# A two-block transformer kernel on one core: the split weights of every stage placed 64 bytes further on in their buffers

## The reference, cut to what matters

```
for l in range(DEPTH):                                   # DEPTH = 2
    h = rmsnorm(x, mix_norm[l]);  p = h @ w_in[l]        # 1024 x 1440
    x = x + mixers(p) @ w_o[l]                           # 1024 x 1024
    h = rmsnorm(x, ffn_norm[l])
    x = x + (silu(h @ w_gate[l]) * (h @ w_up[l])) @ w_down[l]   # 1024 x 2816, 2816 x 1024
...
# second model, for the context (256 rows) and for the latents (512 rows)
y = mixer_ab(modulate(h))          # h @ ab_w_in (4112 columns) ... @ ab_w_out
h = (silu(g) * u) @ ffn_w_out      # g, u = split(h @ ffn_w_in), 2816 wide, per layer
y = mixer_c(...)                   # h @ attn_w_qkv, joint attention, @ attn_w_out
```

## Time and profile before

| | us |
|---|---|
| runs | 3002.12, 3000.85, 3006.8 |
| median | 3002.12 |
| the profiled execution | 3006.76 |
| its span in the trace | 3004.9 |
| PE busy in the span | 2942.4 (98%) |
| POOL, DVE, ACT busy | 1310.1, 1824.1, 1265.7 |

### The profile page before, as it was taken

One profiled execution on the slowest core, in us unless ns is written; L12 is line 12 of the kernel. 1 busy time (PEld: TensorE's weight loads), 2 busy tenths in 40 slices (PEclk: granted clock), 3 DMA queues, 4 the chain that ended last, 5 costly groups with the idle time before them and its releaser, 6 DMA issues.

```text
span 3004.9 us, 43067 instructions
## 1 busy us (share of the span) xinstructions
PE 2942.4 (98%) x16850; PEld 2479.0 (82%) x16850; DVE 1824.1 (61%) x3001; ACT 1265.7 (42%) x2026; POOL 1310.1 (44%) x687
## 2 busy tenths in 40 slices
PE   8999999999999999999999999999999999999999
PEld 7668888786788888778888998878788788889998
DVE  5656777856563553655327867666775567474445
ACT  4643222246444333225336655542223435454445
POOL 4323444532276334333444454444444330176665
PEclk9999999999999999999999999999999999999999
DMA  7224554522245223223333433445554210123332
GB/s 136 67 65 123 172 174 148 178 62 74 75 134 151 88 71 91 78 69 110 116 105 93 117 116 112 140 127 169 182 171 131 96 64 11 43 64 106 99 106 78
DMA packets 468697, 323.92 MB, mean 108 GB/s; under 512 B 90264, under 2 KB 435488, under 8 KB 467984
## 3 DMA queue, kind: packets, MB, share of 16 engines
q1 hardware_dynamic: 463728, 309.55, 35.0%
q0 software_dynamic: 2112, 5.32, 0.6%
q10 hardware_dynamic: 2656, 6.30, 0.6%
HBM read 315.85 MB, written 5.24 MB: 107 GB/s over the span
## 4 chain that ended last, share of the span: by engine, by line
PE 88%; DVE 7%; POOL 2%; ACT 2%; issue 1%; DMA 1%; POOLq 0%; DVEq 0%; ACTq 0%
PE G L3350 13%; PE G L3359 10%; PE G L3360 10%; PE G L3364 10%; PE G L3606 4%; PE G L3607 4%; PE G L3611 4%; PE G L3627 2%; PE G L3631 2%; PE G L3628 2%; PE G L4687 1%; PE G L3674 1%; PE G L3669 1%; PE G L3670 1%; POOL WL L844 1%; PE G L3379 1%
## 5 line engine op out<-in xcount | busy, mean ns | idle before, releaser
L844 POOL TENSOR_TENSOR WL<-raw,WH 128x1024 fp32r<-128x1024 f32 (+2 forms) x454 | 1051.7, 2338 | 1491.0 <-ACT WH L925 1491.0
L925 ACT ACTIVATE WH<-raw 128x1024 fp32r<-128x1024 f32 (+2 forms) x454 | 431.8, 999 | 471.9 <-PE G L3611 304.9
L3359 PE MATMUL G<-hH,WH 128*128 128x512 f32 x1216 | 476.9, 392 | 0.7 <-ACT xtok L1783 0.7
L3360 PE MATMUL G<-hL,WH 128*128 128x512 f32 x1216 | 473.6, 389 | 0.0
L1997 DVE SCALAR_TENSOR_TENSOR acc<-adaw,cvec,acc 128x512 f32<-128x512 f32 x280 | 285.8, 1073 | 4.2
L3364 PE MATMUL G<-hH,WL 128*128 128x512 f32 x1216 | 287.9, 389 | 0.0
L3359 PEld LDWEIGHTS G<-hH,WH 128*128 128x128 f32 x1216 | 228.2, 188 | 52.7 <-issue 3.3
L3364 PEld LDWEIGHTS G<-hH,WL 128*128 128x128 f32 x1216 | 228.2, 188 | 47.4
L3360 PEld LDWEIGHTS G<-hL,WH 128*128 128x128 f32 x1216 | 228.3, 188 | 46.6
L2026 DVE TENSOR_TENSOR FH<-silu,G 128x512 fp32r<-128x512 f32 x44 | 30.3, 688 | 233.6 <-PE G L3364 178.1
L896 POOL TENSOR_TENSOR WL<-raw,WH 128x512 fp32r<-128x512 f32 x101 | 129.4, 1298 | 85.5 <-ACT WH L1048 85.4
(11 more groups left out here) (887 smaller groups left out, 6919.8 us busy)
## 6 DMA issues: line engine op xcount, KB each, us to landing
raw<-ffn_w_in_in SPq DMA_DIRECT2D x264, 256.0 KB, 3.4
adaw<-ada_w_in SPq DMA_DIRECT2D x48, 1024.0 KB, 5.2
raw<-ab_w_in_in SPq DMA_DIRECT2D x128, 256.0 KB, 3.0
raw<-ffn_w_out_in SPq DMA_DIRECT2D x96, 256.0 KB, 3.0
raw<-w_gate_in SPq DMA_DIRECT2D x88, 256.0 KB, 3.3
raw<-w_up_in SPq DMA_DIRECT2D x88, 256.0 KB, 3.4
raw<-w_down_in SPq DMA_DIRECT2D x64, 256.0 KB, 2.9
raw<-w_in_in SPq DMA_DIRECT2D x40, 256.0 KB, 3.4
```

Source lines behind the costliest of these rows:

```text
L844: nc.gpsimd.tensor_tensor(low(c)[:, cut], raw[c % 2][:, cut], high(c)[:, cut].bitcast(F32), ALU.subtract)\
L925: nc.scalar.activation(high(c)[:, cut], raw[c % 2][:, cut], ACT.Copy).then_inc(weights_hi, 1)
L3359: mm(dst, view(high(c), k), xh, start=(k == 0 and not (joint and i)), stop=False)
L3360: mm(dst, view(high(c), k), xl, start=False, stop=False)
```

## The change

All chunks, in every stage, lie at columns 16 to 2063 of their buffers. `high` and `low` lose their case, the table `beside` goes, the blocks of the last feed-forward (`block_of`) move by `SIDE`, and the three places that named `WH` and `WL` directly go through `high` and `low`. What is written there (ACT's copies, POOL's and DVE's differences) and what is read (PE's stationary operands, or moving ones where the factors are exchanged) moves by 64 bytes; `raw`, the transfers, the activations and all results stay where they are. Every engine has the same instructions with the same waits in the same order as before: 10,020 matmuls, 513 ACT copies, 494 POOL and 19 DVE subtractions have another address in them, and the chunks of `c` and `k` have none.

```diff
         def block_of(buffers, c, b):
 
             i = turn_of[c, b]
-            return buffers[(seven_from + i // 4) % 2][:, i % 4 * BLOCK:i % 4 * BLOCK + BLOCK]
+            return buffers[(seven_from + i // 4) % 2][:, SIDE + i % 4 * BLOCK:SIDE + i % 4 * BLOCK + BLOCK]
...
-        beside = {first[name] + i for name, n, _ in names if name[0] in "ck" for i in range(n)}
 
         def high(c):
-            return WH[c % 2][:, SIDE:SIDE + SLOT] if c in beside else WH[c % 2][:, 0:SLOT]
+            return WH[c % 2][:, SIDE:SIDE + SLOT]
 
         def low(c):
-            return WL[c % 2][:, SIDE:SIDE + SLOT] if c in beside else WL[c % 2][:, 0:SLOT]
+            return WL[c % 2][:, SIDE:SIDE + SLOT]
...
-                    for j, (x, y) in enumerate(((WH, hH), (WH, hL), (WL, hH))):
-                        last = mm(G[b][:, :], view(x[c % 2], k), y[:, k, :], start=(k == NH // 2 and j == 0), stop=(k == NH // 2 - 1 and j == 2))
+                    for j, (x, y) in enumerate(((high(c), hH), (high(c), hL), (low(c), hH))):
+                        last = mm(G[b][:, :], view(x, k), y[:, k, :], start=(k == NH // 2 and j == 0), stop=(k == NH // 2 - 1 and j == 2))
...
```

More of the change, by code:

```diff
@@ L4503, in last_out @@
                 for q in range(KD):
-                    for j, (x, y) in enumerate(((WH, hH), (WH, hL), (WL, hH))):
-                        last = mm(out_bank(n, k)[:, :], view(x[c % 2], q), y[:, q, :], start=(q == 0 and j == 0), stop=(q == KD - 1 and j == 2))
+                    for j, (x, y) in enumerate(((high(c), hH), (high(c), hL), (low(c), hH))):
+                        last = mm(out_bank(n, k)[:, :], view(x, q), y[:, q, :], start=(q == 0 and j == 0), stop=(q == KD - 1 and j == 2))
                     if q == KD - 2:
@@ L4694, in joint_out @@
                 for k in ks:
-                    for j, (x, y) in enumerate(((WH, hH), (WH, hL), (WL, hH))):
-                        last = mm(G[b][:, :], view(x[co % 2], k), y[:, k, :], start=(k == 0 and j == 0), stop=(k == KD - 1 and j == 2))
+                    for j, (x, y) in enumerate(((high(co), hH), (high(co), hL), (low(co), hH))):
+                        last = mm(G[b][:, :], view(x, k), y[:, k, :], start=(k == 0 and j == 0), stop=(k == KD - 1 and j == 2))
                 if KD - 1 in ks:
```

## The result

The changed kernel takes 3036.36 us (median of four runs, 3031.96 to 3042.69), beside 3002.46 us for the kernel before: 1.0107 times as long, 95% interval 1.0088 to 1.0126. The forecast was 2991 and the range ended at 3004. What happened is rival 2, in all of the long products and at a higher price than it had been given, while the seven-product tiles gained nearly what was forecast.

A forecast was written before the change was run, and what follows sets the result against it. PE, busy 98% of the span, was taken as the bound. Terms 10.5 + 1.5 + 0 + 0 = 12.0 us off the median 3002.12 gave 2990.1, forecast as 2991 us allowing one slow long run; range 2983 to 3004.

The forecast's parts named there:

- rival 2: In 512-column runs, share s stays some 4.7 ns slower, losing 36 s us against a gain of 12; chance 0.13.
- seven-product tiles: Last feed-forward, 1,596 matmuls with 256 moving columns: from 120.0 to 113.1 ns, saving 10.5 us; bounds 3.5 to 11.0.
- The 512-column products: 7,680 matmuls with stationary weights throughout the kernel: change taken as 0, gain at most 7.7 us, loss 36 to 38.
- The step's other end: Loss bound for the 7,680 matmuls of 512 columns: some 5 ns each, 36 to 38 us.
- the slow pace of `c`: Context's 256-column blocks with weights at column 16: 117.8 ns a matmul against 113.1 at the fast pace, 4.7 ns more.
- Rival 3: Whole kernel: nothing changes, the 120 ns belong to the tiles' operands, not the weights' place; time 3002; chance 0.10.
- rival 1: Last feed-forward's tiles lock into the slow pace, saving 3.5 us, moving weights saving 1.5: 2997; chance 0.21.
- The moving weights: 672 matmuls in which 256 columns of weights move: 283 to 279 ns duration, saving 1.5 us; bounds 0 and 2.7.
- The writers: ACT, POOL and DVE writing to column 16: 0 on ACT, no loss on POOL, DVE indifferent; covered by PE anyway.

The follow-up runs named there:

- bench1: TensorE alone, weights and moving data placed at varying distances: 512 columns took 226.7 ns at 0, 233.3 at 16; 256 columns 120.0 at 0, 113.3 or 117.8 at 16.
- bench3: TensorE alone, 256-column runs with weights 16 or 19 columns ahead, entered directly from 512-column runs with weights at 0 or 16; 113.3 or 117.8 ns.
- with_downs: Kernel before with last feed-forward's weight blocks and seven token chunks at column 16, down products' moving data also 64 bytes on: 3000.98 us, ratio 0.9988.
- nineteen: Kernel before with last feed-forward's blocks, context's weights and down products' moving data at column 19, token chunks at 16: 2995.12 us, ratio 0.9959.
- the first of its parts: Kernel before with only the last feed-forward's weight blocks moved to column 16: 2996.65 us, ratio 0.9975.

## Why the prediction was wrong, and where it was right

**The 512-column products: the step that failed.** "I take 0, since 388 against 389 is the row nearest to the case." show that a weight load under a long product adds 1 ns at most to its duration at column 0. They say nothing about another distance, and the distance turned out to be what matters: bench1 has the same load of 188 ns at 226.7 and at 233.3. The step's other end, "some 5 ns", from the slow pace of `c` and the beginning of a run, was the right one, and a little low: 6.2 ns by the traces, 47.6 us and not 36 to 38. (The 7,680 leave out 24 products in the latents' columns, 0.15 us.) These rows of run-ins were in plain sight: a pace of 232 ns exists at column 0 too, for the first five, before the run comes to 226. At 16 columns in bench1 all four entries stay at 233.3.

**The argument that chose it.** 0 was taken because long products "leave no mark" of the load while short ones do, as if a place that is bad for short products could only be better elsewhere. The distance 0 is the best of all that were run for 512 columns (one entry at 4 was as fast) and among the worst for 256, so that the row on the one had no bearing on the other.

**Rival 2** named the mechanism, its sign from s = 0.33 and the place where it would show ("blocks of 16 at 3.70 us or 393 ns in `b0` and `t`"); they came at 3.73 and 395. Its chance, 0.13, was too low for a term of 7,680 matmuls that no row of before showed in its new state. Its case "3026 with all of them" was short by 6.2 - 4.7 ns on 7,680, 11.5 us.

**Rival 3**, and the rule beside it, fell. The Trainium skill, in "TensorE: Matmul & The Clock Gate", Part 2: What happens when you issue a matmul, has moving data and weights come through two independent ports. By that rule the place of the weights would change nothing, and the runs here disagree at both widths: in the two kernels, with the same data in the same order, the weights' move by 64 bytes took the long products from 227.1 to 233.3 ns and the tiles from 120.0 to 113.3 or 117.8.

**The tiles** went as forecast: 9.6 us against 10.5, with three of four long runs at 113.3 ns; the prediction allowed for one at 117.8. The ground for it was wrong in part. Only three of the four runs are entered out of down products. The first one follows the gate and up products that stand at the start of the stage, and its dense part begins after waits on DVE, here in after:

```profile
2725.64 0.69 DVE WL L2108
...
2726.38 0.74 PE G L3630 x4
```

It is the one that went at 117.8. For the three others what they are entered from matters (bench3), and that is luck here: they went at 113.3 behind down products at 233.3. Had the down products stayed at 226.9, as the prediction took them to, the three would by `with_downs` and bench3 have gone at 117.8, and the tiles would have saved 3.5 to 4.5 us, about what rival 1 has.

**The moving weights** went nearly as forecast, 1.9 us against 1.5, most of them at 117.8 ns. **The writers** cost nothing, as forecast: the busy times above, and the benches without them.

**Open.** That two reads meet, of moving data and of the weights loaded under them, is argued and not shown. Dense products that need no new weights, at two distances, would test it and were not run. The runs show that the distance within 256 bytes decides, and by how much, for each width; that it is not all shows in `nineteen`, where distance 0 took 229.3 ns.

## What to carry to other kernels

A placing that helps products of one width must be measured for every other width that it touches, and a term with many instructions and no row in its new state deserves its bound, not zero. Keep each width's own distance between weights and moving data: here 0 for 512 columns and 19 (or 16) columns for 256. If a change is cheap to split by width, split it first: the first of its parts here was worth 0.25%, the other cost 1.26%.

## What the runs showed of the hardware that was not expected

The pace of dense split matmuls depends on the distance within 256 bytes between where weights and moving data begin: 226.7 to 234 ns with 512 columns, 113.3 to 123.5 with 256, and at the four distances that were run (0, 16, 32 and 48 columns) not at all with 192 (111.7) and 320 (146.7).

A run of 256 columns at 16 has two paces, 113.3 and 117.8 ns, and keeps the one that it was entered with, for up to 503 matmuls: 117.8 in eight of eight behind long products at 226.7, 113.3 in four of eight behind long ones at 233.3. At 19 columns it came to 113.3 within two to six matmuls in all sixteen, and within some eight in the kernel's three long runs behind down products, though some of its short runs in the context kept 120.0.
